# Moving the normalisation of the sample rows from VectorE to GpSimd, and picking and storing them first

## The chip, the cores and the metric

The kernel runs on one core of one Trainium2 chip. The metric is the device time of one execution in microseconds (us); of several runs the median is taken.

## What is computed

One decoder layer for two request groups with the same weights: a prompt of 512 rows and a sample group of 8 x 4 = 32 rows, each row 1024 wide. Modulated RMS norm, one input projection, a short convolution and a dilated attention, an output projection; then a hierarchical mixture of experts, and a last norm. What matters here is the second half:

```
mod = silu(c) @ w_ada + b_ada ;  sh1, sc1, gt1, sh2, sc2, gt2 = split(mod, 6)
x   = x + gt1 * mixed
h2  = rmsnorm(x, norm2_g) * (1 + sc2) + sh2          # the rows this case is about
g   = argmax(h2 @ w_rg + b_rg)                       # one of 4 groups
top = top_k(h2 @ w_re + b_re within g, 2)            # 2 of its 4 experts
out = sum over the two: weight * w2_e( silu(h2 @ w1_e) * (h2 @ w3_e) )
x   = x + gt2 * out
```

Every row goes to 2 of 16 experts. All is f32.

## The kernel before

The 544 rows lie in five tiles: 0 to 3 are the prompt's, 128 rows each, and `TILES` (4) is the sample's, 32 rows. Each engine has its own instruction stream, ordered by semaphores written out by hand; within an engine instructions run in the order of the code. The SP queue issues most loads and stores, GpSimd's queue the indirect gathers.

The kernel has three stages. The first (up to about 810 us) makes the projections, convolution, attention and the output projection. The second, routing (about 812 to 837 us), is where the change lies. The third runs the experts: rows sorted by expert are taken in tiles of 96 slots, two tiles to a pair; for each tile TensorE multiplies by w1 and w3 (line 1375, `inner`) and by w2 (line 1388, `outer`) while the weights `e` of the next experts are loaded by SP and the rows `xg` of the next tile are gathered by GpSimd (line 2655, `rows_of`) from `x_tok` in HBM, which holds all rows of h2.

Routing goes like this:

- `xa` holds the rows before their division by the root, multiplied by the norm's gains. ScalarE takes the root (line 1698), VectorE its reciprocal `rstd` (line 2238), which counts `rec_done` up to 2.
- TensorE folds the partial logits (line 1319). VectorE then works out the two experts of every row in thirty small instructions, lines 2240 to 2291, most of them on 128 partitions x 5 to 80 elements. On the way it signals `rt_dve` twice. The last one writes `chosen`, and `oh_done` tells TensorE, which counts positions with it (lines 1341 and 1342). VectorE copies the counts and makes `first` (line 2303), the one-hot matrix that picks the 96 rows of the first expert's tile, and with it `slot_done`.
- h2 of tiles 2 and 3 is made by TensorE (lines 1331 and 1334, diag(rstd) times xa plus the shift) and copied to SBUF by ScalarE (line 1714, `h2_act`). For tile 3 the products wait for the first `rt_dve`, because VectorE reads logits from one of their banks. h2 of tiles 0, 1 and `TILES` is made by VectorE in `normed(tt)` (line 2252, `h2_done`), one instruction each, after `first`.
- TensorE picks: for each tile in `PICK_ORDER` it waits for the tile's h2 and issues twelve products, `first` x h2 (line 1354; 24 matmul instructions in the profile), which add up over the tiles in three banks. In the last tile each bank signals `xgT_pe`; VectorE transposes the banks into `xs` (line 2325), the input of the first expert.
- SP stores the five tiles of h2 to `x_tok` in the same order (line 866, `xz_out`). GpSimd's first gather waits for all five.

The shift of the modulation lies in `tokt[:, 1]` for the prompt and in `toks[:, 1]` for the sample rows; both came with `rows_in`. `qb_done` is a semaphore that GpSimd uses in the attention stage; it stands at 3 x 3 x 4 = 36 when routing begins. GpSimd does nothing in routing before its first gather.

Of the kernel before, what the change touches and what calls it, by code (L numbers as in the profile page):

```python
# [19 lines left out]
ALU = mybir.AluOpType  # L20
# [3 lines left out]
P = 128  # L24
D = 1024
# [3 lines left out]
NS = DEC_B * DEC_T  # L29
NT = SEQ + NS  # L30
HALF = NT // 2
TILES = SEQ // P
HD = 64
HEADS = 8
GROUPS = 3
AC = HEADS * HD // P
# [15 lines left out]
GROUPS32 = TG * 2 * MAX_PAIRS  # L52
TABLE = 32

PICK_ORDER = (2, 3, 0, 1, TILES)
COUNT_STEPS = -(-NT // TS) - 1

COL_Q = 3 * D
# [38 lines left out]
def _build(nc, x_prompt, x_sample, cache_k1, cache_v1, cache_k2, cache_v2, cache_k3, cache_v3,  # L97
# [48 lines left out]
    rstd = keep("rstd", [P, 8])  # L146
# [18 lines left out]
    r = Region(oT_at)  # L165
# [3 lines left out]
    r = Region(c_region)  # L169
# [10 lines left out]
    r = Region(keep.at)  # L180
# [20 lines left out]
    r = Region(rope_at)  # L201
# [7 lines left out]
    r = Region(kvr2_at)  # L209
# [17 lines left out]
    r = Region(kTs_at)  # L227
# [11 lines left out]
    r = Region(c_region)  # L239
# [11 lines left out]
    r = Region(x2_at)  # L251
    x2 = r("x2", [P, TILES + 1, D])
    tokt_at = r.at
    tokt = r("tokt", [P, 3, D])
# [5 lines left out]
    r = Region(toks_at)  # L260
    toks = r("toks", [NS, 3, D])
# [15 lines left out]
    r = Region(h2_at)  # L277
    h2 = r("h2", [P, TILES + 1, 4, DQ])
# [15 lines left out]
    r = Region(oT_at)  # L294
    e13_0 = r("e13_0", [P, 2, KC, DE])
    e2_0 = r("e2_0", [P, FC, D])
    xa = Region(r.at)("xa", [P, TILES + 1, D])
# [21 lines left out]
    r = Region(h2_at)  # L319
# [10 lines left out]
    r = Region(base + P * 4)  # L330
# [15 lines left out]
    r = Region(h2T_at)  # L346
# [15 lines left out]
    r = Region(xg_end)  # L362
# [3 lines left out]
    r = Region(toks_at)  # L366
# [3 lines left out]
    r = Region(tokt_at)  # L370
    tw = r("tw", [P, 2, 5, 2, GROUPS32])
    assert r.at <= tokt_at + 2 * D * 4
    r = Region(oT_at)
# [82 lines left out]
    for g in (2, 1):  # L456
        rows_g = WINDOWS[g] - DEC_T
        parts = 4 if g == 2 else 1
        n = rows_g // parts
# [88 lines left out]
    def quarters(src):  # L548

        return src.rearrange("p (r c) -> p r c", r=4)  # L550

    with ExitStack() as ctx:
        def sem(name):
            return ctx.enter_context(nc.semaphore(name))
# [21 lines left out]
        rec_done = sem("rec_done")  # L576
# [11 lines left out]
        rope_done = sem("rope_done")  # L588
        h2_pe = sem("h2_pe")
        qb_done = sem("qb_done")  # L590
        kt_pe = sem("kt_pe")
        kt_ev = sem("kt_ev")
        vt_pe = sem("vt_pe")
# [52 lines left out]
        rows_in = sem("rows_in")  # L646
        wr_pad = sem("wr_pad")
        ss2_done = sem("ss2_done")
        h2_done = sem("h2_done")
        xa_done = sem("xa_done")  # L650
        xaT_pe = sem("xaT_pe")
        h2_act = sem("h2_act")
# [68 lines left out]
        def _(sp):  # L721
# [125 lines left out]
            def load_e2(q, e):  # L847

                for half in range(2):
                    sp.dma_start(half_lines(e2[q], half), half_source(w2_v, e, half)).then_inc(e2_in[q], 16)  # L850
# [11 lines left out]
            load_e2(1, 1)  # L862
            for i, tt in enumerate(PICK_ORDER):
                n = P if tt < TILES else NS
                sp.wait_ge(*((h2_act, i + 1) if i < 2 else (h2_done, i - 1)))
                sp.dma_start(x_tok[1 + P * tt:1 + P * tt + n], h2[0:n, tt].rearrange("p r c -> p (r c)"))\
                    .then_inc(xz_out, 16)
            def next_w13(jp, q, e):
# [68 lines left out]
        def _(pe):  # L937
# [173 lines left out]
            def scores_s(x):  # L1111

                w, cp = k_steps[x]
                half, _, g, _ = kv_units[w]
                n = kv_tiles(w)
                out = psum[:, 2 + w % 2, :]
                if cp == 0 and w >= 2:
                    pe.wait_ge(ss_mx, w - 1)
                if n == 1:
                    for g_ in range(GROUPS):  # L1120
                        for ch in range(AC):
                            pe.matmul(out[:, P + NS * g_:P + NS * g_ + NS], QB[:, g_, ch, 4 * half:4 * half + 4, :],
                                      kTn[:, g_, ch, :], start=(ch == 0), stop=(ch == AC - 1))
                for i in range(2):
                    pe.wait_ge((ktr_act, ktr_dve)[i], x + 1)
                    for ch in (2 * cp + i,) if n == 2 else (2 * i, 2 * i + 1):
                        for j in range(4):
                            at = 1024 * i + 256 * j if n == 2 else 512 * ch + P * j
                            mm = pe.matmul(out[NS * j:NS * j + NS, 0:P * n], QB[:, g, ch, 4 * half + j, :],  # L1129
                                           kTs[:, at:at + P * n], start=(ch == 0), stop=(ch == AC - 1))  # L1130
                if cp == 1 or n == 1:
                    mm.then_inc(ss_pe, 1)
# [183 lines left out]
            for tt in range(TILES + 1):  # L1316
                n = P if tt < TILES else NS
# [21 lines left out]
            for tt in range(TILES + 1):  # L1339
                n = P if tt < TILES else NS  # L1340
# [7 lines left out]
            pe.wait_ge(slot_done, 1)  # L1348
            for i, tt in enumerate(PICK_ORDER):
                n = P if tt < TILES else NS  # L1350
                pe.wait_ge(*((h2_act, i + 1) if i < 2 else (h2_done, i - 1)))
                for g in range(TG):
                    for r_ in range(4):
                        mm = pe.matmul(psum[32 * r_:32 * r_ + 32, 5 + g, 0:DQ], first[0:n, tt, 32 * g:32 * g + 32],  # L1354
                                       h2[0:n, tt, r_, :], start=(i == 0), stop=(i == TILES))
                    if i == TILES:
                        mm.then_inc(xgT_pe, 1)

            pe.wait_ge(moved_act, 3)
            for g in range(TG):  # L1360
                for tt in range(TILES + 1):
                    n = P if tt < TILES else NS
# [431 lines left out]
        def _(dve):  # L1794
            local = [0]

            def own(ins):

                local[0] += 1
                ins.then_inc(dve_local, 1)  # L1800
                dve.wait_ge(dve_local, local[0])
# [223 lines left out]
            for G in range(2 * C0):  # L2025
# [6 lines left out]
                if misc_use(G, 0):  # L2032
                    c, j = divmod(m - 2, 9)
                    g = j // 3
                    n = GROUPS * c + g
# [17 lines left out]
                if u:  # L2053
                    n, c, a = u
# [3 lines left out]
                if u:  # L2058
                    n, c, a = u
# [120 lines left out]
            for m in range(D0, N_P):  # L2180
# [6 lines left out]
                for t in range(2):  # L2187
                    dve.wait_ge(grp, 2 * m + t + 1)
                    n = HALF if t == 0 else SEQ - HALF
# [39 lines left out]
            for tt in range(3, TILES + 1):  # L2229
                n = P if tt < TILES else NS  # L2230
# [16 lines left out]
            dve.wait_ge(rec_done, 2)  # L2247

            def normed(tt):
                n = P if tt < TILES else NS  # L2250
                shift = (tokt if tt < TILES else toks)[0:n, 1, :]
                dve.scalar_tensor_tensor(h2[0:n, tt, :, :], quarters(xa[0:n, tt, :]), rstd[0:n, tt:tt + 1],
                                         quarters(shift), ALU.mult, ALU.add).then_inc(h2_done, 1)

            dve.wait_ge(lg_pe, 1)
            own(dve.tensor_tensor(lg[:, 0:TILES, :],
# [43 lines left out]
            def rows_chosen(out, e):  # L2300
# [5 lines left out]

            rows_chosen(first, 0)
            normed(0)
            rows_chosen(early, 1)
            normed(1)  # L2310
            normed(TILES)
            own(dve.tensor_tensor(cmp6[:, :, :], counted[:, 80:96].unsqueeze(2).to_broadcast([P, NE, COUNT_STEPS]),
                                  cst[:, 8:8 + COUNT_STEPS].unsqueeze(1).to_broadcast([P, NE, COUNT_STEPS]), ALU.is_gt))
            own(dve.tensor_reduce(ends[:, 0], cmp6[:, :, :], AX.X, ALU.add))
# [265 lines left out]
        def _(pool):  # L2580
# [13 lines left out]
            for G in range(2 * B_P + 8):  # L2594
# [14 lines left out]
                if t == 0 and 1 <= m and m - 1 < B_P and kind(m - 1) in "qk":  # L2609

                    c, j = divmod(m - 1, 9)
# [13 lines left out]
                if t == 1 and 2 <= m < B_P + 2 and kind(m - 2) in "kv":  # L2625
                    c, j = divmod(m - 2, 9)
                    g = j // 3
                    n = GROUPS * c + g
# [24 lines left out]
            def rows_of(q, g):  # L2653

                pool.indirect_dma_start(xg[:, q, g, :], None, x_pieces,  # L2655
                                        bass.IndirectOffsetOnAxis(piece[:, q, g:g + 1], 0)).then_inc(xg_in[q], 16)

            pool.wait_ge(xz_out, ZEROED + 16 * (TILES + 1))
            pool.wait_ge(xgT_pe, TG)
            pool.wait_ge(piece_done, 1)  # L2660
# [147 lines left out]
```

## Time and profile before

| | us |
|---|---|
| median of 3 runs (lowest, highest) | 1119.56 (1118.93, 1120.02) |
| the profiled execution | 1120.83 |
| its span | 1119.0 |
| TensorE, VectorE, ScalarE, GpSimd busy | 1088.7, 551.5, 361.8, 171.6 |
| mean granted clock of TensorE | 0.999 of full |

The profile is of one execution. Starts are counted from the start of the span; the execution's own time is 1.8 us longer than the span. In a timeline row stand the start, the time to the end of the group, the engine, the line, the operation, what it writes and reads with its shape, the count, and in brackets how long the engine stood idle before it and for whom. PE is TensorE's products, PEld its weight loads, DVE VectorE, ACT ScalarE, POOL GpSimd, SPq SP's queue.

### The profile page before, as it was taken

The numbers are of one execution on the slowest core, as the hardware profiler recorded it, in microseconds if no ns is written. First come the engines' busy times: TensorE is split into PE (matmuls) and PEld (weight loads), VectorE is DVE, ScalarE is ACT, GpSimd is POOL, SyncE is SP. The second block draws the span as 40 slices with busy tenths as digits, with TensorE's granted clock in tenths as the row PEclk, the third lists the DMA queues.
The fourth block names the chain that finished last, engine by engine and source line by source line (L and its number), as shares of the span: only waits on it lengthen the run. The fifth ranks groups of instructions, "written<-read, shape, count | busy, mean of one in ns | idle before, by whom it ended". The sixth has DMA issues, their size and how long they took to land.

```text
span 1119.0 us, 28889 instructions
## 1 busy us (share of the span) xinstructions
PE 1088.7 (97%) x12093; PEld 938.5 (84%) x12093; DVE 551.5 (49%) x1226; ACT 361.8 (32%) x658; POOL 171.6 (15%) x242
## 2 busy tenths in 40 slices
PE   4999999999999999999999999999999999999997
PEld 4899999999999998898779999999966677777753
DVE  1845565565665654444445444434576332333326
ACT  5623333333333332332235444442241211111112
POOL 1334323233231200000000000000002112121111
PEclk9999999999999999999999999999999999999999
DMA  9969979989967737656989888629788999999996
GB/s 348 340 193 349 360 262 360 342 278 359 330 244 284 240 112 277 208 186 210 360 342 378 272 281 309 235 79 313 291 308 342 343 420 420 422 423 425 423 394 240
DMA packets 161815, 344.17 MB, mean 308 GB/s; under 512 B 11627, under 2 KB 116507, under 8 KB 147182
## 3 DMA queue, kind: packets, MB, share of 16 engines
q1 hardware_dynamic: 149086, 318.90, 77.4%
q0 software_dynamic: 5808, 16.05, 4.0%
q10 hardware_dynamic: 6832, 7.93, 2.1%
q8 instruction: 68, 1.11, 0.4%
q14 instruction: 21, 0.17, 0.0%
HBM read 322.08 MB, written 108.85 MB: 385 GB/s over the span
## 4 chain that ended last, share of the span: by engine, by line
PE 91%; DMA 3%; DVE 2%; ACT 2%; issue 1%; POOL 1%; another core or an unknown queue 0%; SPq 0%; POOLq 0%; DVEq 0%
PE psum L1029 51%; PE psum L1375 13%; PE psum L1388 7%; PE psum L1107 3%; DMA e<-in_w_dram 2%; PE psum L1073 2%; PE psum L1085 2%; PE psum L1094 2%; PE psum L952 2%; PE psum L1129 2%; PE psum L1156 1%; PE psum L1050 1%; DMA sttok<-in_state_conv_dram 1%; PE psum L1473 1%; PE psum L1354 1%
## 5 line engine op out<-in xcount | busy, mean ns | idle before, releaser
L1029 PE MATMUL psum<-hHi,whi 128*128 128x272 f32 x1200 | 353.4, 294 | 0.3 <-ACT rb L1644 0.3
L1029 PE MATMUL psum<-hLo,whi 128*128 128x272 f32 x1200 | 346.4, 289 | 0.0
L1029 PE MATMUL psum<-hHi,wlo 128*128 128x272 f32 x1200 | 345.3, 288 | 0.0
L1029 PEld LDWEIGHTS psum<-hHi,whi 128*128 128x128 f32 x1200 | 226.1, 188 | 10.8 <-issue 9.9
L1029 PEld LDWEIGHTS psum<-hHi,wlo 128*128 128x128 f32 x1200 | 226.2, 188 | 0.0
L1029 PEld LDWEIGHTS psum<-hLo,whi 128*128 128x128 f32 x1200 | 225.6, 188 | 0.0
L1375 PE MATMUL psum<-e,xs 128*32 128x256 f32 x3072 | 170.7, 379 | 0.9 <-issue 0.8
L1818 DVE TENSOR_TENSOR wlo<-wraw,whi 128x1024 fp32r<-128x1024 f32 x100 | 133.7, 1338 | 73.4 <-ACT whi L1546 73.0
L1375 PEld LDWEIGHTS psum<-e,xs 128*32 128x32 f32 x3072 | 116.1, 110 | 52.0 <-issue 3.2
L1546 ACT ACTIVATE whi<-wraw 128x1024 fp32r<-128x1024 f32 x100 | 104.9, 1051 | 23.0 <-PE psum L1029 22.9
L2655 POOL DMA_INDIRECT xg<-x_tok,piece x45 | 43.0, 956 | 434.5 <-DMA x_tok<-h 248.4
L1388 PE MATMUL psum<-e,hT 128*32 128x256 f32 x1440 | 81.1, 379 | 1.6 <-DMA e<-in_w_dram 0.8
L1747 ACT ACTIVATE sil<-psum 128x128 f32<-128x128 f32 x48 | 13.2, 278 | 201.0 <-PE psum L1375 193.6
L1388 PEld LDWEIGHTS psum<-e,hT 128*32 128x32 f32 x1440 | 56.0, 110 | 24.1 <-issue 1.7
L2448 DVE TENSOR_TENSOR hid<-sil,psum 128x128 f32<-128x128 f32 x48 | 13.7, 286 | 120.3 <-ACT sil L1747 113.0
L2604 POOL TENSOR_TENSOR t<-rb,ropec 128x272 f32<-128x272 f32 x48 | 38.9, 810 | 188.4 <-ACT rb L1644 166.9
L1644 ACT ACTIVATE rb<-psum 128x272 f32<-128x272 f32 x48 | 18.8, 393 | 103.9 <-PE psum L1029 103.9
L1984 DVE COPY kTs<-psum 128x1024 f32<-128x1024 f32 x18 | 22.1, 1225 | 47.6 <-PE psum L1107 47.6
L1620 ACT ACTIVATE pr<-pr,nb 128x768 f32<-128x768 f32 x32 | 30.0, 938 | 47.7 <-DVE nb L2071 47.1
L2606 POOL TENSOR_TENSOR shb<-shb,ropes 128x272 f32<-128x272 f32 x48 | 41.7, 868 | 1.5 <-DVE shb L2098 1.5
L1029 PE MATMUL psum<-mixHi,whi 128*128 128x272 f32 x128 | 37.5, 293 | 0.0
L1029 PE MATMUL psum<-ybHi,whi 128*128 128x272 f32 x128 | 37.1, 290 | 0.0
(390 smaller groups left out, 1560.9 us busy)
## 6 DMA issues: line engine op xcount, KB each, us to landing
e<-in_w_dram SPq DMA_DIRECT2D x96, 1024.0 KB
wraw<-in_w_in_dram SPq DMA_DIRECT2D x76, 512.0 KB, 6.1
out_dram<-in_cache_k_dram SPq DMA_DIRECT2D x32, 1022.0 KB, 9.7
out_dram<-in_cache_v_dram SPq DMA_DIRECT2D x32, 1022.0 KB, 8.1
adar<-in_w_ada_dram SPq DMA_DIRECT2D x36, 512.0 KB, 7.5
kvr<-in_cache_k_dram SPq DMA_DIRECT2D x8, 2048.0 KB, 7.9
kvr<-in_cache_v_dram SPq DMA_DIRECT2D x8, 2048.0 KB, 10.2
out_dram<-in_cache_k_dram SPq DMA_DIRECT2D x8, 1016.0 KB, 8.7
```

The costliest lines, as they stand in the source:

```text
L952: mm = pe.matmul(psum[NS * j:NS * j + NS, bank, 0:P], cT[:, k, :], ring[:, k // 2, k % 2, P * j:P * j + P], start=(k == 0), stop=(k == KC ...
L1029: mm = pe.matmul(psum[:, t, 0:HALF], w[:, slot, k, :], x[:, k, cols], start=(k == 0 and n == 0), stop=(k == k_n - 1 and n == 2))
L1073: mm = pe.matmul(out, qT[rows_h, c % 2, g, P * a:P * a + P], kT[rows_h, c % 2, g, keys], start=True, stop=True)
L1107: mm = pe.transpose(turned[:, at:at + P], kvr[:, w % 2, j, 512 * r_ + P * ch:512 * r_ + P * ch + P], ident[:, :])
L1375: mm = pe.matmul(psum[32 * n:32 * n + 32, g, 0:2 * P].rearrange("p (w f) -> p w f", w=2), xs[:, q, k, 32 * g:32 * g + 32], (e13[q] if w13 ...
L1388: mm = pe.matmul((psum[:, 3 + g, 0:DQ] if u else first_y(g))[32 * n:32 * n + 32], hT[:, fc, 32 * g:32 * g + 32], w2_[:, fc, DQ * n:DQ * n ...
L1546: act.activation(whi[:, slot], wraw[:, slot], ACT.Copy).then_inc(hi_done, 1)
L1620: act.activation(pr[:, h], pr[:, h], ACT.Exp, bias=nb[:, h:h + 1], scale=SCALE, accum_out=rs[:, h:h + 1]).then_inc(s_exp, 1)
L1818: dve.tensor_tensor(wlo[:, slot], wraw[:, slot], whi[:, slot].bitcast(F32), ALU.subtract)\
L2604: pool.tensor_tensor(t1[:, t, :], rb[:, t, :], ropec[:, cols], ALU.mult).then_inc(rot_done, 1)
L2606: pool.tensor_tensor(shb[:, t, :], shb[:, t, :], ropes[:, cols], ALU.mult)\
L2655: pool.indirect_dma_start(xg[:, q, g, :], None, x_pieces, bass.IndirectOffsetOnAxis(piece[:, q, g:g + 1], 0)).then_inc(xg_in[q], 16)
```

## The change

GpSimd makes h2 of the sample rows in two instructions, product and sum, as soon as `rstd` is there; the second waits for the first, and each counts `qb_done`. VectorE no longer does `normed(TILES)`. TensorE picks from the sample tile first and SP stores it first; both wait for `qb_done` at 38. For the other tiles the waits are the same, written by tile number.

```diff
-PICK_ORDER = (2, 3, 0, 1, TILES)
+PICK_ORDER = (TILES, 2, 3, 0, 1)
...
+        QB_ALL = 3 * GROUPS * AC
...
             for i, tt in enumerate(PICK_ORDER):
                 n = P if tt < TILES else NS
-                sp.wait_ge(*((h2_act, i + 1) if i < 2 else (h2_done, i - 1)))
+                sp.wait_ge(*((qb_done, QB_ALL + 2) if tt == TILES else (h2_act, tt - 1) if tt >= 2 else (h2_done, tt + 1)))
                 sp.dma_start(x_tok[1 + P * tt:1 + P * tt + n], h2[0:n, tt].rearrange("p r c -> p (r c)"))\
                     .then_inc(xz_out, 16)
...
             for i, tt in enumerate(PICK_ORDER):
                 n = P if tt < TILES else NS
-                pe.wait_ge(*((h2_act, i + 1) if i < 2 else (h2_done, i - 1)))
+                pe.wait_ge(*((qb_done, QB_ALL + 2) if tt == TILES else (h2_act, tt - 1) if tt >= 2 else (h2_done, tt + 1)))
...
             def normed(tt):
-                n = P if tt < TILES else NS
-                shift = (tokt if tt < TILES else toks)[0:n, 1, :]
-                dve.scalar_tensor_tensor(h2[0:n, tt, :, :], quarters(xa[0:n, tt, :]), rstd[0:n, tt:tt + 1],
-                                         quarters(shift), ALU.mult, ALU.add).then_inc(h2_done, 1)
+                dve.scalar_tensor_tensor(h2[:, tt, :, :], quarters(xa[:, tt, :]), rstd[:, tt:tt + 1],
+                                         quarters(tokt[:, 1, :]), ALU.mult, ALU.add).then_inc(h2_done, 1)
...
             rows_chosen(early, 1)
             normed(1)
-            normed(TILES)
...
+            pool.wait_ge(rows_in, 32)
+            pool.wait_ge(rec_done, 2)
+            h2_s = h2[0:NS, TILES, :, :].rearrange("p r c -> p (r c)")
+            pool.tensor_tensor(h2_s, xa[0:NS, TILES, :], rstd[0:NS, TILES:TILES + 1].to_broadcast([NS, D]), ALU.mult)\
+                .then_inc(qb_done, 1)
+            pool.wait_ge(qb_done, QB_ALL + 1)
+            pool.tensor_tensor(h2_s, h2_s, toks[:, 1, :], ALU.add).then_inc(qb_done, 1)
             pool.wait_ge(xz_out, ZEROED + 16 * (TILES + 1))
```

## Rows read from the trace of the kernel before

**Rows 1.** The page: busy us, share of the span and instructions by engine.

```profile
PE 1088.7 (97%) x12093; PEld 938.5 (84%) x12093; DVE 551.5 (49%) x1226; ACT 361.8 (32%) x658; POOL 171.6 (15%) x242
```

**Rows 2.** The chain that ended last, from 826: start us, us, what.

```profile
826.80 0.86 PE psum L1331 x2
...
829.52 6.82 PE psum L1354 x120
...
837.20 10.50 PE psum L1375 x192
```

**Rows 3.** Timeline 819 to 828: start us, us, engine, line, operation.

```profile
819.46 0.20 DVE L2238 RECIPROCAL rstd<-rstd 128x8 f32<-128x8 f32 x1
...
820.22 0.23 DVE L2244 CAST tri_b<-tri 128x128 bf16<-128x128 f32 x1
820.48 0.43 DVE L2245 TENSOR_TENSOR upto<-cst 128x256 f32<-128x256 f32 x1
...
821.59 0.24 DVE L2256 TENSOR_TENSOR lg<-psum,rstd 128x80 f32<-128x80 f32 x1 [0.68 <-PE psum L1319]
821.86 0.24 DVE L2259 TENSOR_TENSOR lg<-lg,brb 128x80 f32<-128x80 f32 x1
...
823.24 0.18 DVE L2272 TENSOR_TENSOR rt<-rt,rs 128x20 f32<-128x20 f32 x1
...
827.38 0.24 DVE L2291 TENSOR_TENSOR chosen<-onehot 128x80 bf16<-128x80 f32 x1
827.67 0.10 PEld L1341 LDWEIGHTS psum<-chosen,tri_b 128*128 128x128 bf16 x1 [0.85 <-DVE chosen L2291]
```

**Rows 4.** The same timeline from 831 to 836.

```profile
831.35 1.28 DVE L2252 SCALAR_TENSOR_TENSOR h<-xa,rstd,tokt 128x1024 f32<-128x1024 f32 x1
...
832.55 1.27 DVE L2252 SCALAR_TENSOR_TENSOR h<-xa,rstd,toks 32x1024 f32<-32x1024 f32 x1
...
834.84 1.02 PEld L1354 LDWEIGHTS psum<-h,first 32*32 32x32 f32 x24 [0.41 <-issue]
835.61 1.24 DVE L2325 STREAM_TRANSPOSE xs<-psum 128x256 f32<-128x256 f32 x3 [0.46 <-PE psum L1354]
```

**Rows 5.** The same timeline: stores of h2 and first gathers.

```profile
826.17 8.00 SPq L866 DMA_DIRECT2D x_tok<-h  x5
...
840.15 1.07 POOL L2655 DMA_INDIRECT xg<-x_tok,piece  x1 [248.36 <-DMA x_tok<-h]
...
842.83 0.98 POOL L2655 DMA_INDIRECT xg<-x_tok,piece  x1 [1.61 <-PE psum L1375]
```

**Rows 6.** GpSimd: one line (ns min/median/max), one group (busy us, mean ns).

```profile
L2604 POOL TENSOR_TENSOR t<-rb,ropec x48: 762/771/1755, 44.9 to 336.8; 128x272 f32<-128x272 f32 x48
...
L2624 POOL COPY kTn<-kT 128x32 f32<-128x32 f32 x12 | 2.5, 206 | 18.3 <-DVE kT L1933 18.3
```

**Rows 7.** Instructions of L1818, ns min/median/max: up to 340 and after.

```profile
L1818 DVE TENSOR_TENSOR wlo<-wraw,whi x38: 1159/1672/1790, 43.4 to 337.7; 128x1024 fp32r<-128x1024 f32 x38
...
L1818 DVE TENSOR_TENSOR wlo<-wraw,whi x22: 1215/1223/1226, 345.5 to 557.1; 128x1024 fp32r<-128x1024 f32 x22
```

**Rows 8.** Timeline 100 to 112, of VectorE and then of GpSimd.

```profile
108.22 0.69 DVE L2077 TENSOR_SCALAR pr<-pr,ri 128x768 f32<-128x768 f32 x1
...
111.14 1.69 DVE L1818 TENSOR_TENSOR wlo<-wraw,whi 128x1024 fp32r<-128x1024 f32 x1
...
108.45 1.09 POOL L2606 TENSOR_TENSOR shb<-shb,ropes 128x272 f32<-128x272 f32 x1
...
110.97 0.79 POOL L2606 TENSOR_TENSOR shb<-shb,ropes 128x272 f32<-128x272 f32 x1
```

**Rows 9.** Stretches: PE, PEld, DVE, ACT, POOL busy; PEclk, DMA share, GB/s.

```profile
838.00:840.00 2.00, 2.00 (x44) 1.21 (x40) 1.76 (x8) 0.00 (x0) 0.00 (x0) 1.00 0.03 12
840.00:842.00 2.00, 2.00 (x44) 1.23 (x40) 1.57 (x10) 0.00 (x0) 1.07 (x1) 1.00 0.10 25
```

**Rows 10.** The same by stretch, near the end.

```profile
1112.00:1115.00 3.00, 0.32 (x3) 0.19 (x1) 2.88 (x6) 1.56 (x4) 0.00 (x0) 1.00 0.69 283
```

## The prediction, made before the changed kernel had run

> **What bounds the kernel now.** I began with the page [rows 1]: TensorE is busy for 97% of the span, so an edit counts by what it does to the times at which TensorE may go on. Next the chain of waits through the routing stage [rows 2]: it is TensorE nearly everywhere, through the products that make h2 of tiles 2 and 3 (lines 1331 and 1334, the last ends at 826.80 + 0.86, about 827.65), 6.82 us of picks, to the first expert product at 837.20. The same stretch on VectorE [rows 3] shows how tight it is: `chosen` ends at 827.38 + 0.24 = 827.62, and TensorE loads it at 827.67, as soon as its own products have ended. Two chains reach that point together: TensorE's, and thirty small VectorE instructions (counted in the code) from `rstd` (819.46 + 0.20 = 819.66) on. Whatever delays VectorE's chain delays TensorE nearly in full.
>
> **What the edit takes away.** `normed(TILES)` leaves VectorE: 1.27 us from 832.55, ending at 833.82 [rows 4]. Does anyone wait for it? TensorE's picks of the sample rows come last; their weight loads start at 834.84, 1.0 us after that end, and the 0.41 us in front of them are put down to "issue", not to VectorE. The 120 picks take 6.82 us [rows 2], about 1.3 a tile. The sample tile begins at a change of shape (32 rows instead of 128), and that change remains in the new place. I cost the reorder at 0 (bounds: 0, and a gain of those 0.4). Behind `normed(TILES)` VectorE has four small instructions and then waits 0.46 us for the picks; with 1.3 us freed it waits 1.7 us. No gain: what hides the work is the picks themselves, which bound the stage. In the new order tile 1 is last; its rows, ready at 831.35 + 1.28 = 832.63, are wanted after four tiles, at 829.52 + 5.2 = 834.7. No stall.
>
> The last store moves from the sample tile (ready 833.82) to tile 1 (832.63), and GpSimd's first gather, at 840.15, is the one that waits for a store [rows 5]. It may come up to 1.2 us earlier, but the second gather waits for TensorE (842.83), and the transposes into `xs` need all three. Cost and gain 0.
>
> **What it adds.** Two GpSimd instructions over 32 x 1024 f32, each reading two SBUF tensors, issued when `rstd` is ready; the second waits for the first. The trace before has no such shape. The nearest [rows 6]: 128 x 272 f32 with two inputs, 0.762 at least, median 0.771; a copy of 128 x 32 takes 0.206. Lower bound: all of that copy is fixed cost, (0.765 - 0.206) / 272 = 2.06 ns an element, so 0.206 + 1024 x 0.00206 = 2.31 us. Upper bound: no fixed cost, 0.765 x 1024 / 272 = 2.88. I take 2.4, near the lower end, because a copy of a few elements still costs 0.2. The Trainium skill ("GPSIMD Engine Reference", § 3.1) gives 4497 ns for a two-input f32 operation of 2048 elements; an estimate between that figure and this row is 2.35 us, and it would change the sum below by 0.1.
>
> As mere work they are hidden: 819.74 to 822.15 and on to about 825, long before the picks (829.5) want them. What is not hidden is what they do to VectorE. `wlo` (L1818, two SBUF inputs) has a median of 1.672 us in the stage in which GpSimd works and 1.223 after it [rows 7]. One case [rows 8]: GpSimd's L2606 runs from 110.97 to 111.76; L1818, issued at 111.14, takes 1.69, so 0.47 of it was standing, until 111.61, 0.15 us before GpSimd's reported end. The other way round, L2606 at 108.45 takes 1.09 instead of 0.77 behind a TENSOR_SCALAR that ran from 108.22 to 108.91. So whoever comes second waits for the whole of the other's instruction.
>
> The Trainium skill ("SBUF — State Buffer", § Who interferes with whom) has the same rule: the port pair is an exclusive lock, and VectorE wants it with two SBUF inputs or in a 2-port mode (copy, cast, tensor_scalar). By that page an instruction with one SBUF input passes. It speaks against this change, and by it the sum is the one below.
>
> Step by step, with 2.4 us each and a release 0.15 before the end. GpSimd's first: 819.66 + 0.08 for the semaphore (`chosen` to its load took 0.05) = 819.74 to 822.15, release 822.0. VectorE's cast L2244 (820.22, 0.23; one input, counted among the held because the one-input TENSOR_SCALAR of rows 8 collided too) or at the latest L2245 (820.48, two inputs, 0.43) stands until 822.0. After the cast L2245 asks at about 822.2, and so does GpSimd's second: a toss-up.
> - VectorE first: L2245 until 822.63; GpSimd's second from about 822.5 to 824.9, release 824.75. L2256 reads PSUM and one SBUF tensor; if it passes, L2259 (two inputs) asks at 822.9 and stands until 824.75, instead of starting at 821.86: 2.9 us late. If L2256 is held itself: 824.75 instead of 821.59, 3.15.
> - GpSimd first: 822.2 to 824.6, release 824.5; L2245 then until 824.9, L2256 starts at 824.94 instead of 821.59: 3.35 us late.
>
> If only L2245 and not the cast is held, 2.7. With 2.31 us an instruction the two orders give 2.7 and 3.15, with 2.88 they give 3.8 and 4.3. I take 3.1, between the two orders. From there the chain has no GpSimd beside it and keeps its lengths: `chosen` is ready at 830.7 instead of 827.62. TensorE's second half of the h2 products waits for VectorE's `rt_dve`, after L2272 (823.42 [rows 3], then 826.5); it has three pairs of 0.86 [rows 2] to do, until 829.1, and idles until 830.7. So the path is 3.1 us later, in full. ScalarE's first exponential and, behind it, its copy of tile 2 wait for the same signal; the copy ends near 828, and the picks want it after 832.6. SP's queue: all five stores now stand behind GpSimd's second instruction (about 825) and behind them the next weight loads; the first store went out at 826.17 before [rows 5], and the loads wait for TensorE. Cost 0. GpSimd's gathers stand behind both instructions, at 840: cost 0.
>
> **Does it reach the end?** From 838 to 842 the DMA engines are 3 and 10% busy [rows 9]: what was loaded ahead has landed, and every later load, gather and store is released by TensorE's progress. So all after 837 shifts as one, full queues later on included, and no slack gives it back. Sum: 0 (removed) + 3.1 (VectorE held) + 0 (stores, gathers) = +3.1. Against the profiled execution's own time, 1120.83 (span 1119.0 and 1.8 around it), that is 1123.9; that execution is 1.3 above the median of the runs, 1119.56, on which the forecast rests: 1122.7.
>
> **Rivals.** No change can't be told from 0.2%, 2.2 us.
> - GpSimd does not hold VectorE here (32 partitions only, small VectorE operands): then 0, at best -0.4, so 1119.5. For it: no row has such a pair. Against: rows 7 and 8, and the median over 38 instructions. It decides if no VectorE instruction between 819.7 and 825 stands; then TensorE's products end last, as now. This is the case on the other side: not slower. Chance 0.12.
> - Only one of the two collides (VectorE slips its two-input instructions in between, or GpSimd starts late): 2.3 less what of it falls in VectorE's own wait before L2256 (0.68 [rows 3]), +1.6, so 1121.2. Chance 0.08.
> - The clock. TensorE gets holes of 1.4 us (at 825), 1.6 (829) and 1 (832) within some 7. In 1112 to 1115 it was busy for 0.32 of 3 us, and the granted clock was still 1.00 [rows 10]; I expect it kept. If it fell to the lower level, 1.2 instead of 2.4 GHz, the picks' 6.8 us would double: +10, 1129.6. Chance 0.03.
> - Faster by more than 2.2 us: nothing in the rows is that long. 0.02 is left for what I don't see.
>
> **Numbers.** The forecast's own case (both collide) has 0.75, and its own range is 1121.9 (2.7 less 0.4) to 1124.2 (4.3, and 0.3 of scatter). For 8 in 10 I take in the single collision: 1120.6 to 1124.2. Slower by over 0.2%: 0.74 of the main case and the clock's 0.03, 0.77. Within: 0.21. Faster: 0.02.
>
> **What would show it.** In the profile after: two GpSimd rows of 2.3 to 2.9 us from 819.7 on; L2244 or L2245 with 1.5 to 2 us instead of 0.23 or 0.43, and L2245 or L2259 with 1.8 or more; `chosen` near 830.7; TensorE's idle time in front of L1341 put down to VectorE, 1.5 us or so; picks 6.4 to 6.9 us; the first expert product near 840.3. I am wrong if the small VectorE instructions keep their 0.2 us beside GpSimd, if GpSimd's are much shorter than 2.3 us, or if the shift at 837 does not stand at the end.

## The result, and the profile after

| | before | after |
|---|---|---|
| median of 12 runs each (lowest, highest), us | 1119.60 (1117.73, 1123.71) | 1124.78 (1120.48, 1130.33) |
| ratio of the times, 95% interval | | 1.0044 (1.0031 to 1.0056) |
| the profiled execution, its span | 1120.83, 1119.0 | 1122.62, 1120.5 |

Slower by 0.44%, 5 us. The forecast was 1122.7, and its range ended at 1124.2: right in direction, 2 us too little. Two things stand out. The changed kernel scatters over 10 us, the kernel before over 6. And the profiled execution, one of the quicker ones, is only 1.8 us longer than the profiled one of before. So the profile alone can't show the whole of it.

The first lines of the profile page after: TensorE is busy for as long as before (1088.7 us), over a longer span [rows 1].

```profile
span 1120.5 us, 28890 instructions
...
PE 1088.6 (97%) x12093; PEld 939.4 (84%) x12093; DVE 553.4 (49%) x1225; ACT 361.5 (32%) x658; POOL 176.1 (16%) x244
```

The timeline after, routing (columns as in [rows 3]; the line numbers are 1 higher than before up to about 2250, then 1 or more lower):

```profile
820.77 0.20 DVE L2239 RECIPROCAL rstd<-rstd 128x8 f32<-128x8 f32 x1
...
821.05 0.24 DVE L2242 TENSOR_SCALAR hilo<-cst 128x5 bf16<-128x5 f32 x1
821.15 1.88 POOL L2659 TENSOR_TENSOR h<-xa,rstd 32x1024 f32<-32x1024 f32 x1 [228.15 <-DVE rstd L2239]
821.32 1.75 DVE L2243 CAST hilo<-cst 128x5 bf16<-128x5 f32 x1
...
823.11 0.23 DVE L2245 CAST tri_b<-tri 128x128 bf16<-128x128 f32 x1
823.12 2.41 POOL L2662 TENSOR_TENSOR h<-h,toks 32x1024 f32<-32x1024 f32 x1
...
823.37 2.45 DVE L2246 TENSOR_TENSOR upto<-cst 128x256 f32<-128x256 f32 x1
...
825.86 0.24 DVE L2255 TENSOR_TENSOR lg<-psum,rstd 128x80 f32<-128x80 f32 x1
...
827.89 1.10 PE L1332 MATMUL psum<-xa,diag 128*128 128x512 f32 x2 [1.50 <-DVEq L2275]
...
831.64 0.24 DVE L2290 TENSOR_TENSOR chosen<-onehot 128x80 bf16<-128x80 f32 x1
...
831.93 0.18 PE L1342 MATMUL psum<-chosen,tri_b 128*128 128x16 bf16 x1 [1.23 <-DVE chosen L2290]
...
833.78 6.81 PE L1355 MATMUL psum<-h,first 32*32 32x256 f32 x120 [0.19 <-DVE first L2302]
...
839.87 1.24 DVE L2323 STREAM_TRANSPOSE xs<-psum 128x256 f32<-128x256 f32 x3 [1.65 <-PE psum L1355]
...
841.39 4.96 PE L1376 MATMUL psum<-e,xs 128*32 128x256 f32 x88
...
842.80 1.08 POOL L2653 DMA_INDIRECT xg<-x_tok,piece  x1 [17.27 <-DVE piece L2327]
```

Read it from `rstd`, which this execution reached 1.31 us later than the one of before. (In front of a stretch of lower clock, 478.1 to 481.5, in the attention stage, TensorE was 0.4 us ahead of the execution before, and behind it 1.2 us late; this has nothing to do with routing.) GpSimd's product starts 0.18 us after VectorE's reciprocal has ended. VectorE's TENSOR_SCALAR of line 2242 is already running and passes; the cast of line 2243, 0.18 us before, takes 1.75; the cast of line 2245 slips in between GpSimd's two instructions; line 2246, 0.43 us before, takes 2.45. From `rstd` (start) to L2255 it is 5.09 us, before 821.59 - 819.46 = 2.13: 2.96 us late. `chosen` starts 10.87 us after `rstd`, before 7.92: the same 2.95. TensorE shows two new holes, stretches in which it stands: 1.50 us in front of line 1332 and 1.23 in front of line 1342, the latter for `chosen`; between them it works for 2.8 us. The picks take 6.81 us against 6.82 in the old order. From `rstd` to the first expert product it is 841.39 - 820.77 = 20.62 us; before, 837.13 - 819.46 = 17.67 by the same timeline. The difference is 2.95 us; the forecast was 3.1. VectorE now waits 1.65 us for the picks before `xs` instead of 0.46 [rows 4]: that is where the 1.3 us taken off it went. The first gather starts 1.41 us after the first product instead of 3.0 [rows 5]; nobody needed that.

After that the two profiled executions differ by chance: from the first expert product to the last product of all it takes about 272 us in this one and 275 in that of before. TensorE's stops between 865 and 895 add up to 1.5 us in the profile before and to 0.5 in this one; in the second profiles of the two kernels they are 0.9 (e1_before) and 3.0 (e2_after). What is left to explain is the median: 5 us, of which 2.95 are seen.

### The profile page after: what moved, and what is told of

It reads as the page before. It is cut to its first block and busy times, and to the rows that moved or that the text cites. A ratio compares the mean times of both kernels' runs of the same rounds, so it can differ in the third digit from the quotient of the medians.

```text
span 1120.5 us, 28890 instructions
## 1 busy us (share of the span) xinstructions
PE 1088.6 (97%) x12093; PEld 939.4 (84%) x12093; DVE 553.4 (49%) x1225; ACT 361.5 (32%) x658; POOL 176.1 (16%) x244
## 5 line engine op out<-in xcount | busy, mean ns | idle before, releaser
L1108 PEld LDWEIGHTS psum<-ident,kvr 128*128 128x128 f32 x288 | 32.1, 143 | 6.6 <-issue 6.6
```

What stands on the lines that cost most here:

```text
L1108: mm = pe.transpose(turned[:, at:at + P], kvr[:, w % 2, j, 512 * r_ + P * ch:512 * r_ + P * ch + P], ident[:, :])
```

## Experiments

Each run also gives the mean clock that was granted to TensorE, and runs with a lower clock were longer. Over all groups of runs of the two kernels (82 runs of before with a clock listed, 25 of the changed kernel):

| mean granted clock | before: runs | changed: runs |
|---|---|---|
| 0.998 and 0.999 | 69, median 1119.3 us | 10, median 1122.0 us |
| 0.997 | 12, median 1120.6 us | 3, median 1123.8 us |
| 0.994 to 0.996 | 1 | 12, median 1125.5 us |

At a good clock the changed kernel is 2.7 us slower, close to what the trace shows for routing. Half of its runs have a lower clock and are 3.4 us longer still. The theory from here on: VectorE's standing (2.95 us) plus, in about half of the runs, a stretch of lower clock that the new holes in TensorE's work bring on. The rivals: the extra lies in other work, or in GpSimd's work as such, or the clock falls at random.

The runs come from two chips: e1 to e4 and 47 of the runs of before from one, e5 to e11 and 35 of before from the other; for the first 12 of the changed kernel the chip isn't listed. The chips differ. On the first, 12 of the 47 runs of before had 0.997 or less, on the second 1 of 35. So clocks are compared best on one chip. On the first, 1 of 47 runs of before is at 0.996 or less, and 11 of 36 of the three kernels whose VectorE is 3 us late (e2, e3, e4). That is far from chance (about 1 in 3000), and e4 is one of them, in which GpSimd does nothing in routing. A count of low runs misses some: e9_write_only had a stretch of low clock in routing and a mean of 0.998.

The main measure of each profile is the time from the start of `rstd` to the first expert product. The time from there to the last product is in the last column but one; it varies by 3 us between two profiles of one kernel (after and e2_after) and shows no tie to the first.

| kernel | rstd to first expert product, us | more than before | median us (runs) | of them at 0.996 or less | from there to the end of products | ratio, 95% interval |
|---|---|---|---|---|---|---|
| before | 17.67 | | | | 274.9 | |
| e1_before | 17.7 | 0 | 1120.08 (12) | 0 | 272.9 | 1.000 (0.9988 to 1.0013) |
| after | 20.62 | 2.95 | 1124.78 (12) | 5 | 272.2 | 1.0044 (1.0031 to 1.0056) |
| e2_after | 20.63 | 2.96 | 1124.25 (12) | 6 | 275.5 | 1.0035 (1.0019 to 1.0050) |
| e3_old_order | 20.64 | 2.97 | 1122.27 (12) | 2 | 273.3 | 1.0025 (1.0009 to 1.0041) |
| e4_vector_late | 20.68 | 3.01 | 1123.03 (12) | 3 | 275.4 | 1.0028 (1.0013 to 1.0043) |
| e5_filled | 20.63 | 2.96 | 1122.26 (11) | 0 | 274.1 | 1.0030 (1.0018 to 1.0042) |
| e6_half | 18.71 | 1.04 | 1120.21 (11) | 1 | 272.6 | 1.0016 (1.0006 to 1.0026) |
| e7_twice_late | 23.85 | 6.18 | 1125.45 (5) | 1 | 273.9 | 1.0055 (1.0042 to 1.0069) |
| e8_after | 23.95 | 6.28 | 1124.07 (1) | 1 | 273.0 | |
| e9_write_only | 20.27 | 2.60 | 1122.06 (1) | 0 | 273.1 | |
| e10_later | 20.00 | 2.33 | 1122.09 (11) | 0 | 273.5 | 1.0020 (1.0011 to 1.0030) |
| e11_last | 20.07 | 2.40 | 1122.86 (1) | 0 | 275.2 | |

(In e7, e8 and e9 the second column holds a stretch of lower clock, see there.)

**The kernel before again, e1_before.** No edit.

> The kernel before, unchanged, to see the granted clock of its runs and whether its short stop of TensorE at 866 to 868 comes back. If the changed kernel's extra 2 us beyond the 2.95 us of routing come from the clock, this kernel's runs show a mean granted clock of 0.998 to 0.999 in nearly all and times within 1118 to 1121; if the chip lowers the clock at random whatever the kernel, they show 0.994 to 0.997 as often as the changed one (8 of its 12).

Measured: 0.997 in one run and 0.998 to 0.999 in 11, times from 1117.72 to 1122.39, a little wider than expected. (Of the changed kernel's first 12 runs seven, not eight, were at 0.994 to 0.997.) Of the 35 runs of the kernel before that stood beside this group ten had 0.997 and one 0.995, the slowest (1124.56); so 0.997 is nothing special on this chip. Its stop at 866 to 868 did not come back in that form; there were stops of 0.20 us at 867.6 and 0.66 at 873.2. So those stops move about by themselves.

**The changed kernel again, e2_after.** No edit.

> The changed kernel again. Both theories expect the routing stage 2.9 to 3.0 us longer (VectorE's L2245 and L2246 standing). The theory that the rest is the clock expects a ratio of 1.004, runs with 0.999 at +1 to +3 us and runs with 0.994 to 0.996 at +6 to +10. The rival, that the rest lies in other work after routing (weights, gathers), expects the same excess at equal clock.

Routing is 2.96 us longer, the ratio 1.0035. Runs at 0.999 (2) had a median of 1122.0, +2.8; those at 0.996 or less (6) lay between 1123.7 and 1128.8, +4.5 to +9.6. That is near what the clock theory had, but its lower end was put at +6; and two runs at 0.998 were slow too (1124.5 and 1124.7), which the rival expects. The stops after 865 were long in its profile (275.5 in the column above), at a granted clock of 1.00; single executions need not agree with the clock.

**The old order of picks and stores, e3_old_order.**

```diff
-PICK_ORDER = (TILES, 2, 3, 0, 1)
+PICK_ORDER = (2, 3, 0, 1, TILES)
```

> GpSimd makes the sample rows, but they are picked and stored last as before. If VectorE's standing is the cause and the order is worth nothing: same as the changed kernel within 0.3 us in the routing stage, ratio 1.004. If the order itself costs or gains (shape change in the picks, stores all behind GpSimd), routing differs by 0.3 us or more.

Routing: 20.64 against 20.63. In routing the order is worth nothing, neither way. The median is 2 us lower than that of e2_after, with 2 of 12 runs at a low clock instead of 6; the intervals overlap, and 12 runs don't settle whether that is more than chance.

**VectorE late by its own work, GpSimd idle, e4_vector_late.** The kernel before, and in front of `dve.wait_ge(lg_pe, 1)`:

```diff
+            for width in (D, D, 3 * DQ):
+                own(dve.scalar_tensor_tensor(h2[0:NS, TILES, :, :].rearrange("p r c -> p (r c)")[:, 0:width], xa[0:NS, TILES, 0:width],
+                                             rstd[0:NS, TILES:TILES + 1], toks[0:NS, 1, 0:width], ALU.mult, ALU.add))
```

> The kernel before with no GpSimd work in routing, and VectorE 2.95 us late at line 2256 by three products of its own (the sample rows made twice and three quarters early, and again in their old place). If the lateness of VectorE's chain explains everything, the holes in TensorE's work and the clock included, this has the changed kernel's time: ratio 1.004 and its spread of clocks, first expert product about 2.9 us later than before. If GpSimd's work costs something besides, this is clearly faster than the changed kernel: +2.9 us, 1.0026, or less.

The timeline of e4_vector_late, VectorE and then TensorE:

```profile
819.20 0.20 DVE L2238 RECIPROCAL rstd<-rstd 128x8 f32<-128x8 f32 x1
...
820.67 3.62 DVE L2256 SCALAR_TENSOR_TENSOR h<-xa,rstd,toks 32x1024 f32<-32x1024 f32 x3
824.33 0.24 DVE L2259 TENSOR_TENSOR lg<-psum,rstd 128x80 f32<-128x80 f32 x1
```

```profile
826.37 1.10 PE L1331 MATMUL psum<-xa,diag 128*128 128x512 f32 x2 [1.56 <-DVEq L2279]
...
832.27 6.81 PE L1354 MATMUL psum<-h,first 128*32 128x256 f32 x120 [0.19 <-DVE first L2306]
...
839.88 2.37 PE L1375 MATMUL psum<-e,xs 128*32 128x256 f32 x40
```

Nothing of GpSimd stands beside this, and the chain is late all the same. The holes and the length of routing are the changed kernel's, and the time is between e3_old_order and e2_after: 1.0028. By the time alone the two expectations, 1.004 and 1.0026, can't be told apart; by routing, +3.01 us, a VectorE that is 3 us late is enough, and GpSimd's work does nothing else that could be seen. 3 of 12 runs had a low clock, also without GpSimd.

**The holes filled, e5_filled.** The changed kernel, and four products that nobody reads:

```diff
+            def filler():
+                for width in (512, 256):
+                    pe.matmul(psum[:, 7, 0:width], ident[:, :], tokt[:, 1, 0:width], start=True, stop=True)
...
                     if i:
+                        if c == 0:
+                            filler()
                         pe.wait_ge(rt_dve, 1)
...
+            filler()
             pe.wait_ge(oh_done, 1)
```

> The changed kernel, and TensorE does four products that nobody reads (128x512 and 128x256, twice, into an unused bank) in front of its two waits for VectorE, some 1.3 us of each hole, so that it hardly stands still. If the holes are what lowers the clock in some runs: mean granted clock 0.997 or more in nearly all runs (the changed kernel had 11 of 24 at 0.996 or less, the kernel before 1 of 47), and a ratio of about 1.003, the 3 us alone. If the low clock has nothing to do with the holes, 4 to 6 of 12 runs are at 0.996 or less, and the ratio stays at 1.004.

The timeline of TensorE in e5_filled; line 1327 is the filler:

```profile
823.98 1.45 PE L1327 MATMUL psum<-tokt,ident 128*128 128x512 f32 x4
825.55 1.12 PE L1339 MATMUL psum<-xa,diag 128*128 128x512 f32 x2
...
828.23 1.45 PE L1327 MATMUL psum<-tokt,ident 128*128 128x512 f32 x4
...
831.55 6.82 PE L1363 MATMUL psum<-h,first 32*32 32x256 f32 x120 [0.19 <-DVE first L2310]
...
839.16 7.11 PE L1384 MATMUL psum<-e,xs 128*32 128x256 f32 x128
```

Routing is as late as in the changed kernel (20.63), since VectorE is. No run of 11 has less than 0.997, where 12 of the changed kernel's 25 do, and the median is 1122.26 against 1124.5 of those 25. This is what the theory expects, but it does not show that the filling did it, because the chips differ: of those 25 runs 12 are from the other chip, for 12 the chip isn't listed, and only one (e8_after) is from this one. On this chip e10_later, with three holes of 1.12, 0.52 and 0.46 us that nothing fills, has none in 11 at 0.996 or less either and a median of 1122.09, and on the other chip e3_old_order, with both holes open, has 1122.27. Against the kernel before in its own group e5_filled is at 1.0030 (1.0018 to 1.0042), which overlaps both ratios of the changed kernel. So whether filling the holes gains anything is not shown; the changed kernel would have to run several times beside it.

**Half the columns on GpSimd, e6_half.** Old order; GpSimd's two instructions over 512 columns, the other 512 by VectorE in the old place. Only GpSimd's lines are shown, with a part of each left out at [...].

```diff
-            pool.tensor_tensor(h2_s, xa[0:NS, TILES, :], rstd[...].to_broadcast([NS, D]), ALU.mult)
+            pool.tensor_tensor(h2_s[:, 0:2 * DQ], xa[0:NS, TILES, 0:2 * DQ], rstd[...].to_broadcast([NS, 2 * DQ]), ALU.mult)
...
-            pool.tensor_tensor(h2_s, h2_s, toks[:, 1, :], ALU.add)
+            pool.tensor_tensor(h2_s[:, 0:2 * DQ], h2_s[:, 0:2 * DQ], toks[:, 1, 0:2 * DQ], ALU.add)
```

> GpSimd makes only columns 0 to 511 of the sample rows, VectorE the other half in the old place; old order of picks. If VectorE stands for as long as GpSimd's instructions last, these are 1.0 and 1.2 us instead of 1.9 and 2.4, line 2255 starts 0.85 us later than before instead of 2.95, and the ratio is 1.001 or less. If any collision costs a fixed amount, the delay stays above 2 us.

The timeline of e6_half, VectorE (lines 2247 to 2259 are the after's 2243 to 2255) and then GpSimd:

```profile
819.62 0.20 DVE L2243 RECIPROCAL rstd<-rstd 128x8 f32<-128x8 f32 x1
...
820.17 0.90 DVE L2247 CAST hilo<-cst 128x5 bf16<-128x5 f32 x1
821.11 0.23 DVE L2249 CAST tri_b<-tri 128x128 bf16<-128x128 f32 x1
821.37 1.37 DVE L2250 TENSOR_TENSOR upto<-cst 128x256 f32<-128x256 f32 x1
822.77 0.24 DVE L2259 TENSOR_TENSOR lg<-psum,rstd 128x80 f32<-128x80 f32 x1
```

```profile
820.00 1.03 POOL L2666 TENSOR_TENSOR h<-xa,rstd 32x512 f32<-32x512 f32 x1 [228.35 <-DVE rstd L2243]
821.12 1.33 POOL L2669 TENSOR_TENSOR h<-h,toks 32x512 f32<-32x512 f32 x1
```

The cast now stands 0.7 us instead of 1.6, the next line 0.9 instead of 2.0: each until GpSimd's instruction is nearly over. Routing +1.04, forecast 0.85: the price goes with the length of GpSimd's instructions, not with their number. The ratio, 1.0016, is above the 1.001 that was expected, which lies within its interval (1.0006 to 1.0026).

**Twice as late, e7_twice_late.** As e4_vector_late, with `for width in (D, D, D, D, D)`.

> The kernel before, VectorE 5.9 us late by five products of its own, no GpSimd work: TensorE's holes are twice as long. Lateness alone gives +5.9 us, ratio 1.0053. If longer holes lower the clock more often, over half of the runs are at 0.996 or less, the ratio is 1.008 or more, and a profile may show the lower clock within 20 us of the holes. If the clock has nothing to do with holes, clocks are as those of the kernel before and the ratio is 1.005.

Rows of e7_twice_late, TensorE's timeline, then stretches (columns as in [rows 9]):

```profile
829.27 1.63 PE L1331 MATMUL psum<-xa,diag 128*128 128x512 f32 x2 [4.45 <-DVEq L2279]
...
835.45 6.82 PE L1354 MATMUL psum<-h,first 128*32 128x256 f32 x120 [0.19 <-DVE first L2306]
```

```profile
828.00:832.00 4.00, 2.73 (x4) 1.31 (x5) 3.26 (x19) 1.13 (x2) 0.00 (x0) 0.71 0.65 271
832.00:836.00 4.00, 3.81 (x27) 1.55 (x29) 2.70 (x9) 0.91 (x2) 0.00 (x0) 0.86 0.10 40
```

The hole before line 1331 is 4.45 us, and the clock did fall in the profile, from 829.7 to 833.1. But it cost only 0.3 us (routing +6.18, `chosen` +5.90): TensorE had three pairs of products to do before its wait for `chosen`, and at the low clock they lasted until that was there, so that the second hole is gone. It was back at full clock when the picks began (6.82 us). The ratio is that of lateness alone, and of 5 runs only one is at 0.996 or less (four at 0.997 or less, where before has 1 of 35 on this chip). Here the expectation failed: a longer hole does not mean a dearer one. In this profile what lay under the low stretch decided.

**A third profile of the changed kernel, e8_after.** No edit.

> The changed kernel once more, for a profile: with a chance near one half it falls into a run with the clock at 0.996 or less, and then shows where. By the clock theory that is within 20 us after the holes of 826 to 833; by the rival anywhere, as at 478 us in its first profile.

Stretches of e8_after, and then its timeline of TensorE:

```profile
core 0: us, PE busy (x) PEld busy (x) DVE busy (x) ACT busy (x) POOL busy (x), PEclk, DMA share, GB/s
824.00:828.00 4.00, 2.69 (x6) 1.06 (x6) 3.26 (x19) 1.13 (x2) 0.00 (x0) 1.00 1.06 418
828.00:832.00 4.00, 2.56 (x25) 1.21 (x28) 2.98 (x9) 1.15 (x2) 0.00 (x0) 0.93 0.68 249
832.00:836.00 4.00, 4.00 (x44) 1.62 (x40) 3.51 (x8) 1.89 (x2) 0.00 (x0) 0.50 0.80 329
836.00:840.00 4.00, 4.00 (x60) 2.07 (x56) 0.00 (x0) 0.00 (x0) 0.00 (x0) 0.72 0.19 76
840.00:844.00 4.00, 4.00 (x79) 2.42 (x71) 2.79 (x11) 0.00 (x0) 0.45 (x1) 1.00 0.00 0
```

```profile
829.37 0.18 PE L1342 MATMUL psum<-chosen,tri_b 128*128 128x16 bf16 x1 [1.25 <-DVE chosen L2290]
...
831.21 10.13 PE L1355 MATMUL psum<-h,first 32*32 32x256 f32 x120 [0.19 <-DVE first L2302]
841.28 0.94 PE L1364 MATMUL psum<-hilo,early 128*128 128x2 bf16 x15
```

This run (mean 0.995) caught it. The clock fell to the lower of its two levels, 1.2 instead of 2.4 GHz, at 831.4, 2.0 us after the second hole, and rose again at 838.2, while TensorE was busy without a break. In the same two stretches of 4 us (824 to 832) TensorE was busy for 2.69 and 2.56 us here, and for 2.50 and 2.56 in e3_old_order's profile, where the clock stayed at 1.00: the same holes lowered it in one execution and not in another. Under it lay the picks: 10.13 us instead of 6.82. That is 3.3 us, and it explains why this routing is 6.28 us longer instead of 2.95; in the first profile of the changed kernel, at a clock of 1.00, the picks took 6.81. The Trainium skill ("TensorE: Matmul & The Clock Gate", Part 1) has it that TensorE's clock goes up and down with its activity. These rows agree: it fell to 0.50 behind two holes and rose under unbroken work.

**GpSimd writes only, e9_write_only.** The two products replaced by four memsets, each with its own wait. The sample rows of h2 are zero here, so this kernel leaves out their part of the expert stage, and only its routing is read.

> The changed kernel with GpSimd's two products replaced by four memsets of the sample rows, one after the other (the sample rows of h2 are zero then, so this leaves their part of the expert work out). They write SBUF and read nothing. If what VectorE waits for is GpSimd's reading, line 2246 (two SBUF inputs) takes 0.43 us also beside them; if any GpSimd instruction holds it, it takes up to one memset more, about 1 us. If the cast of line 2243 needs more than a read, it stands here too.

The timeline of e9_write_only:

```profile
819.71 1.05 DVE L2242 TENSOR_SCALAR hilo<-cst 128x5 bf16<-128x5 f32 x1
819.78 1.94 POOL L2660 MEMSET h<- 32x1024 f32 x2 [228.08 <-DVE rstd L2239]
...
820.79 0.97 DVE L2243 CAST hilo<-cst 128x5 bf16<-128x5 f32 x1
...
821.88 2.02 POOL L2660 MEMSET h<- 32x1024 f32 x2 [0.16 <-POOL h L2660]
822.05 0.42 DVE L2246 TENSOR_TENSOR upto<-cst 128x256 f32<-128x256 f32 x1
```

Line 2242 (a TENSOR_SCALAR, 0.24 otherwise) and the cast of 2243 (0.18) take about 1 us each beside a memset. Line 2246, with two SBUF inputs, takes its 0.42 right beside the third memset. So the cast and the TENSOR_SCALAR collide with a GpSimd instruction that only writes as well, and the product with two inputs does not; what held it in the changed kernel (2.45) is then most likely GpSimd's reading; there is one case of each. The standing made `chosen` 0.96 us late (828.31 - 819.43 = 8.88 against 7.92). The other 1.64 of the 2.60 are the clock: in this profile it was low from 831.7 to 835.1, behind a hole of 0.99 us for `chosen` and the usual 0.19 for `first`, and the picks took 8.45 us.

**Later starts, e10_later and e11_last.** Both with the old order.

```diff
-            pool.wait_ge(rec_done, 2)
+            pool.wait_ge(oh_done, 1)     # e10_later
+            pool.wait_ge(h2_done, 2)     # e11_last
```

> GpSimd makes the sample rows only after VectorE's chain (it waits for oh_done), old order of picks. The chain is not held any more; held are the instruction that makes first (or the first normed) and those behind it. By the rule that whoever comes second waits out the other: chosen on time, the first expert product 1 to 3 us later than before. If this is over 2 us, no place for the two GpSimd instructions in routing is better than the one tried; by the rival that only the long chain of small instructions is sensitive, it is under 0.5 us.

> GpSimd makes the sample rows after VectorE's last normed, old order of picks. Nothing is held before the picks, but the sample rows are ready at 832.6 + 1.9 + 2.4 = 836.9 instead of 833.8 and wanted at 834.8: first expert product about 2.1 us later than before.

The timeline of e10_later:

```profile
827.30 1.88 POOL L2659 TENSOR_TENSOR h<-xa,rstd 32x1024 f32<-32x1024 f32 x1 [235.77 <-DVE chosen L2290]
...
828.11 1.10 DVE L2301 SCALAR_TENSOR_TENSOR lowest<-chosen,counted 128x5 f32<-128x5 bf16 x1
...
829.27 2.86 POOL L2662 TENSOR_TENSOR h<-h,toks 32x1024 f32<-32x1024 f32 x1
829.82 3.40 DVE L2251 SCALAR_TENSOR_TENSOR h<-xa,rstd,tokt 128x1024 f32<-128x1024 f32 x1
```

`chosen` is on time, and now `lowest` (0.17 otherwise) stands for 1.10 and `normed(0)` (1.28) for 3.40. TensorE waits 1.12 us for `first`, then 0.52 and 0.46 for the two normed tiles. Routing +2.33. In e11_last TensorE waits for the sample rows themselves:

```profile
836.40 1.50 PE L1355 MATMUL psum<-h,first 32*32 32x256 f32 x24 [2.31 <-POOL h L2662]
```

Routing +2.40, and the clock fell behind that hole too, at 838.5 (the mean of 836 to 840 was 0.81), here under the first expert products. No start that was tried with all columns on GpSimd costs less than 2.3 us in routing; in the kernel before, VectorE's instruction of 1.27 us cost nothing there, since nobody waited for it. None of the kernels run here beats the kernel before.

## Why the prediction was right in kind and too small

- That nobody waits for `normed(TILES)`, and that the order is worth nothing: right. e3_old_order has the same routing within 0.01 us, and VectorE's freed time turned into waiting (1.65 us before `xs`, forecast 1.7).
- That GpSimd's instruction holds VectorE's for its whole length: right to within 0.15 us, shown by the rows of L2243 and L2246 and by e6_half. Of the two orders it was "GpSimd first". The first GpSimd instruction took 1.88 us, below the lower bound of 2.31 (its second input is one value for each row, repeated; whether that is why was not tested), the second 2.41. The cast that stood was that of line 2242 in the kernel before (2243 after), one ahead of the L2244 that was named. With 2.4 for both the sum for this order was 3.35; measured 2.96. The value taken, 3.1, between the two orders, was off by 0.15, and this closeness is partly luck: the first instruction was put 0.5 us too long, and the toss-up went the longer way.
- That the delay reaches the end, and no slack gives it back: right as far as medians show it. Runs at 0.998 and 0.999 differ by 2.7 us.
- The step that failed is the rival "the clock", which the sum puts at nothing. I wrote "I expect it kept" and gave 0.03, because in 1112 to 1115 the clock was 1.00 with TensorE busy for 0.32 of 3 us [rows 10]. That row shows only that the clock outlasts a hole for a while: it fell some 2 us after the end of that stretch, in [rows 10]'s own execution at 1117.2, 5 us after the last product; in e1_before, the same kernel, it fell at 1112.7, 2.3 us after it. It does not show that a few holes in a row are free. It needed to be a term with its own chance for each run, since executions differ, and not a rival for all runs at once. Measured: a mean clock of 0.996 or less in 12 of 25 runs, and in profiles a price of 3.3 us where the low stretch lies over the picks (e8_after), 1.6 where it is half as long (e9_write_only), 0.3 where TensorE would have waited anyhow (e7_twice_late). The holes were forecast at 1.4, 1.6 and 1 us and measured at 1.50, 1.23 and 0.19; the third, for `first`, is as short in the kernel before. My +10 for it doubled the picks and added the 3.1; the picks didn't double, since the low stretch ended after 6.8 us. A term of about one half times 3.3 would have given 1124.3, but this is hindsight: no row of before had that chance.
- By the mean of the runs: the changed kernel's 25 average 1124.3, the 82 of before 1119.7, a difference of 4.6 us. Mean clocks of 0.9968 and 0.9982 differ by 0.0014 of 1120 us, 1.6 us at full clock. 2.95 + 1.6 = 4.5, an estimate; the median's 5.2 us of the first group has 0.6 more, which lies within the scatter of such a group (e2_after has 1124.25).

What is shown: the standing of VectorE, its price by length, that lateness alone makes the same routing, that low clocks come with the late VectorE (11 of 36 against 1 of 47 on one chip, e4_vector_late without GpSimd among them), and what a low stretch costs where a profile caught it. What stays open: whether filling the holes takes the low clocks away; whether the changed kernel loses its clock more often than e3_old_order and e4_vector_late, which have the same holes (12 of 25 against 5 of 24); and whether the later start of the expert stage has any part in the stops between 865 and 895, which add up to 0.9 and 1.5 us in the two profiles of before and to 0.5 to 3.3 in those of the late kernels.

## What to carry to other kernels

Before giving GpSimd arithmetic, list what VectorE does in the same microseconds: here a cast and the two-input instructions waited until GpSimd's was nearly over, and a cast of 0.18 us took 1.75. Work that nobody waits for is best left on an engine that would wait anyway. And a hole of 1 to 2 us in TensorE's work just ahead of a dense stretch can cost more than itself: count the chance of a lower clock over what follows, and look at the clock of every run and not of one profile. Compare such counts only between runs of one chip.

## What the hardware showed that I had not expected

- GpSimd's product of 32 x 1024 with a repeated value as second input takes 1.88 us, the sum of two full tensors 2.4 (after, e11_last).
- In e9_write_only GpSimd's memset holds VectorE's TENSOR_SCALAR (1.05 us instead of 0.24) and cast (0.97 instead of 0.18), but not its two-input product (0.42).
- TensorE's clock fell behind holes of 1.51 and 1.25 us, with 2.8 us of work between them, in one of three profiles of the same program; it also fell behind single holes (the 0.19 us for `first` aside) of 0.99 (e9_write_only), 2.31 (e11_last) and 4.45 us (e7_twice_late). The low stretches seen ahead of the last product lasted 3.4 us (four profiles) and 6.8 us (one).
- The clock also fell once in the attention stage, at 478 us (after), with TensorE busy by the profile: all of 470 to 478 and of 478 to 482.
